# Mixer output read once into the weight buffer, output projection by token chunks, sums of the second norm made during the projection

## What is computed

```
cq, ckv, kr, hq, ... = split_projection(h @ lp['w_in'])     # h: modulated rmsnorm of x
o_mla = rmsnorm(mla_attention(...), lp['mla_out_norm'])     # (T, 512)
o_hg  = rmsnorm(o_hg, ...) * silu(hg)                       # (T, 256), gated linear recurrence
o_gla = rmsnorm(o_gla, ...) * silu(gg)                      # (T, 256), gated linear recurrence
mix = jnp.concatenate([o_mla, o_hg, o_gla], axis=-1) @ lp['w_o']
x = x + g1 * mix
h2 = rmsnorm(x, lp['norm_ffn']) * (1.0 + sc2) + sh2
a, u = jnp.split(h2 @ lp['w_ffn_in'], 2, axis=-1)
x = x + g2 * ((jax.nn.silu(a) * u) @ lp['w_ffn_out'])
```

## Time and profile before

| | us |
|---|---|
| median of 3 runs | 3866.0 (3865.39 to 3866.11) |
| the profiled execution's own time | 3858.27 |
| its span, first to last instruction | 3856.5 |
| TensorE busy | 3408.7 |
| VectorE busy | 1475.6 |
| ScalarE busy | 987.9 |
| GpSimd busy | 674.9 |

### The profile page before, as it was taken

One profiled execution on the slowest core, in us unless ns is written; L12 is line 12 of the kernel. 1 busy time (PEld: TensorE's weight loads), 2 busy tenths in 40 slices (PEclk: granted clock), 3 DMA queues, 4 the chain that ended last, 5 costly groups with the idle time before them and its releaser, 6 DMA issues.

```text
span 3856.5 us, 53744 instructions
## 1 busy us (share of the span) xinstructions
PE 3408.7 (88%) x20827; PEld 3059.2 (79%) x20827; DVE 1475.6 (38%) x2528; ACT 987.9 (26%) x2023; POOL 674.9 (18%) x1041
## 2 busy tenths in 40 slices
PE   4799788988959999999948997889879599999998
PEld 3699556766849999999928985567659499999998
DVE  1511345644333433433424104455442344343343
ACT  2421234432131111111123213344330311111110
POOL 0211556531010000000002126475300100000000
PEclk6899889999879999999958998899979799999999
DMA  6144111101200111110141441111021011011111
GB/s 225 43 151 145 53 48 61 38 16 63 78 22 33 44 54 33 54 44 33 33 143 69 153 137 54 44 48 36 18 94 54 11 43 55 33 47 51 33 33 47
DMA packets 194358, 238.29 MB, mean 62 GB/s; under 512 B 20582, under 2 KB 168316, under 8 KB 194204
## 3 DMA queue, kind: packets, MB, share of 16 engines
q1 hardware_dynamic: 163992, 184.07, 15.1%
q0 software_dynamic: 11232, 31.97, 2.4%
q10 hardware_dynamic: 18980, 20.14, 1.7%
HBM read 196.06 MB, written 40.08 MB: 61 GB/s over the span
## 4 chain that ended last, share of the span: by engine, by line
PE 82%; DVE 5%; POOL 3%; ACT 3%; issue 3%; DMA 2%; ACTq 1%; SPq 0%; DVEq 0%; POOLq 0%
PE banks L1282 78%; PE banks L1278 4%; DVE probs_t L2110 1%; ACTq L875 1%; ACT norm_t L858 1%; DVE norm_t L1863 1%; DMA mix_token_major<-mixer_out 1%; DVE act_split L1871 1%; POOL act_split L555 1%; DVE w_split L1846 0%; ACT probs L1113 0%; POOL r_qb L633 0%; POOL r_kb L626 0%; DVE a_stats L2097 0%; DVE r_qb L2016 0%
## 5 line engine op out<-in xcount | busy, mean ns | idle before, releaser
L1282 PE MATMUL banks<-act_split,w_split 128*128 128x384 f32 (+1 forms) x8352 | 1390.8, 328 | 46.0 <-DVE act_split L1871 36.7
L1282 PEld LDWEIGHTS banks<-act_split,w_split 128*128 128x128 f32 x8352 | 1386.1, 189 | 48.3 <-issue 38.1
L1282 PE MATMUL banks<-hidden_split,w_split 128*128 128x384 f32 (+1 forms) x3168 | 528.0, 327 | 0.0
L1282 PEld LDWEIGHTS banks<-hidden_split,w_split 128*128 128x128 f32 x3168 | 524.7, 188 | 0.7 <-DVE hidden_split L2217 0.3
L1880 DVE SCALAR_TENSOR_TENSOR x<-banks,mod,x 128x384 f32<-128x384 f32 (+2 forms) x768 | 354.2, 496 | 231.1 <-PE banks L1282 229.1
L2214 DVE TENSOR_TENSOR hidden_f<-banks,silu_a 128x384 f32<-128x384 f32 x132 | 70.7, 536 | 780.3 <-PE banks L1282 780.3
L1282 PEld LDWEIGHTS banks<-w_split,act_split 128*128 128x128 f32 (+1 forms) x2592 | 315.8, 182 | 16.6 <-issue 10.7
L1282 PE MATMUL banks<-w_split,act_split 128*128 128x264 f32 (+1 forms) x2592 | 326.6, 285 | 0.0
L555 POOL CAST act_split<-norm_t 128x384 fp32r<-128x384 f32 (+1 forms) x96 | 55.0, 572 | 1386.1 <-ACT norm_t L858 1385.4
L1261 ACT ACTIVATE w_split<-w_raw 128x2048 fp32r<-128x2048 f32 x60 | 112.4, 1905 | 383.9 <-PE banks L1282 383.9
L1255 ACT ACTIVATE hidden_split<-hidden_f 128x384 fp32r<-128x384 f32 x132 | 67.0, 508 | 536.5 <-DVE hidden_f L2214 536.5
(11 more groups left out here) (187 smaller groups left out, 3421.9 us busy)
## 6 DMA issues: line engine op xcount, KB each, us to landing
w_raw<-in_w_ffn_in SPq DMA_DIRECT2D x44, 1024.0 KB, 5.1
w_mod_raw<-in_w_mod SPq DMA_DIRECT2D x34, 1024.0 KB, 5.5
w_raw<-in_w_ffn_out SPq DMA_DIRECT2D x22, 1024.0 KB, 4.9
w_mod_first<-in_w_mod ACTq DMA_DIRECT2D x14, 1024.0 KB, 13.7
z_token_major<-z_stage POOLq DMA_DIRECT2D x96, 132.0 KB, 2.1
w_raw<-in_w_in SPq DMA_DIRECT2D x10, 1056.0 KB, 5.8
r_qkg<-z_feature_major SPq DMA_DIRECT2D x16, 576.0 KB, 4.2
r_v<-z_token_major SPq DMA_DIRECT2D x16, 512.0 KB, 3.5
```

Source lines behind the costliest of these rows:

```text
L1282: return T.matmul(out, lhsT, rhs, start=start, stop=stop, skip_group_check=True)
```

## The change

- SyncE loads `mixer_out` while attention still runs: eight tiles into MT, now in slots 1 and 2 of W, each as soon as its store has landed, and of the last tile the recurrence's half into MTR. The last tile's attention half isn't stored and is turned from OM. GpSimd's last `clear` is left out.
- Split 9 is made in the last attention tile, after head 4's copies.
- TensorE turns tiles in the order `MIX`, into banks 4 to 7, five tiles before the projection, two before q = 1 and two before q = 2.
- In the projection the chunk loop is outside the column-tile loop (q = 6m + 2c + ct). Splits 10 and 11 follow q = 2 on VectorE, 12 to 14 follow q = 5, 11 and 17, and split 15 follows the whole norm.
- ScalarE squares each feature tile as soon as its residual is done, GpSimd adds the squares of a chunk up in ACC, and TensorE multiplies the sum once per chunk (`chunk_sum`): chunk 0 after q = 20, the others after q = 23. Chunk 0 is scaled on ScalarE, VectorE and GpSimd ahead of what these do for q = 21 to 23.
- The FFN's wait for a chunk of the norm stands before that chunk's matmuls, inside the loop.

The diff, cut to its core:

```diff
+MIX = [0, 1, 2, 3, 4, 5, 8, 6, 7]
+SQUARED = [q for q in range(24) if q not in (0, 2, 4)]
+MIX_END = ["m2b", "m5b", "m7b"]
...
-    a = [h_at, h_end]
-    MT = place("mix_token_major", [P, 2, D_MODEL], F32, a)
+    MT = place("mix_token_major", [P, NTILE - 1, D_MODEL], F32, [w_at + SLOT * 8, w_end])
+    MTR = place("mix_last", [P, 512], F32, [lt_at, lt_end])
+    SQN = place("norm_sq_n2", [P, 2, 384], F32, [h_at, h_end])
+    TNN = place("norm_t_n2", [P, 2, 384], F32, [h_at + TOK * 4, h_end])
+    ACC = place("norm_sum", [P, 3, 384], F32, [h_at + TOK * 8, h_end])
...
-                sp.wait_ge(a_out, (l + 1) * NTILE * 16)
-                for t, (t0, n) in enumerate(TILES):
-                    if t == 0:
-                        wait(sp, "a_pe", l, f"PV{ORDER[-1]}_7")
-                        wait(sp, "a_dve", l, f"on{ORDER[-1]}")
-                    if t >= 2:
-                        wait(sp, "mix_pe", l, f"m{t - 2}b")
-                    sp.dma_start(MT[0:n, t % 2], mix_d[t0:t0 + n, :]).then_inc(m_ld[t % 2], 16)
+                wait(sp, "a_dve", l, f"qssb{ORDER[-1]}")
+                t0, n = TILES[ORDER[-1]]
+                sp.dma_start(MTR[:], mix_d[t0:t0 + n, 512:1024]).then_inc(m_ld, 16)
+                for i, t in enumerate(ORDER[:-1]):
+                    t0, n = TILES[t]
+                    sp.wait_ge(a_out, (l * (NTILE - 1) + i + 1) * 16)
+                    sp.dma_start(MT[0:n, i], mix_d[t0:t0 + n, :]).then_inc(m_ld, 16)
...
-                out(NTILE - 1)
-                norm_hi("n2", l)
...
+                def add(q):
+                    c, d = q % 6 // 2, 2 * (q // 6) + q % 2
+                    cn = CHUNKS[c][1]
+                    if d:
+                        wait(pool, "n2_act", l, f"sq{q}")
+                        if d > 1:
+                            wait(pool, "n2_pool", l, f"ad{q - 1 if q % 2 else q - 5}")
+                        s.done(V.tensor_tensor(ACC[:, c, 0:cn], ACC[:, c, 0:cn], SQN[:, SQUARED.index(q) % 2, 0:cn], ALU.add),
+                               f"ad{q}")
+
+                def high(c):
+                    c0, cn = CHUNKS[c]
+                    for k in range(KT8):
+                        wait(pool, "n2_act", l, f"h{c}{k}")
+                        s.done(V.tensor_copy(A[:, 0, k, c0:c0 + cn], TNN[:, k % 2, 0:cn]), f"hi{c}{k}")
+
+                for q in range(21):
+                    add(q)
+                high(0)
+                for q in range(21, 24):
+                    add(q)
+                high(1)
+                high(2)
...
+                        if not more and h == 4:
+                            split_hi(l, 9, lambda: wait(act, "r_dve", l, "out8"), 12)
...
+                def square(q):
+                    c, d = q % 6 // 2, 2 * (q // 6) + q % 2
+                    c0, cn = CHUNKS[c]
+                    wait(act, "wo_dve", l, f"o{q}")
+                    out = ACC[:, c, 0:cn]
+                    if d:
+                        j = SQUARED.index(q)
+                        out = SQN[:, j % 2, 0:cn]
+                        if j >= 2:
+                            wait(act, "n2_pool", l, f"ad{SQUARED[j - 2]}")
+                    s.done(S.activation(out, X[:, d, c0:c0 + cn], ACT.Square), f"sq{q}")
+
+                def scaled(c):
+                    cn = CHUNKS[c][1]
+                    wait(act, "n2_pe", l, f"q{c}")
+                    if c:
+                        wait(act, "n2_dve", l, f"t{c - 1}7")
+                    s.done(S.activation(RS[:, 0:cn], ps[6 + c % 2][:, 0:cn], ACT.Ln, bias=EPSC), f"rl{c}")
+                    wait(act, "n2_act", l, f"rl{c}")
+                    s.done(S.activation(RS[:, 0:cn], RS[:, 0:cn], ACT.Exp, scale=-0.5), f"rs{c}")
...
+                for q in range(6, 12):
+                    square(q)
+                split_hi(l, 13, lambda: wait(act, "wo_pe", l, "o11"), 16)
+                for q in range(12, 18):
+                    square(q)
+                split_hi(l, 14, lambda: wait(act, "wo_pe", l, "o17"), 17)
+                for q in range(18, 21):
+                    square(q)
+                scaled(0)
+                for q in range(21, 24):
+                    square(q)
+                scaled(1)
+                scaled(2)
+                split_hi(l, 15, lambda: wait(act, "wo_pe", l, "o23"), 18)
...
+                def mix_turn(t):
+                    n = TILES[t][1]
+                    if t == ORDER[-1]:
+                        wait(pe, "a_dve", l, f"on{t}")
+                    for b in range(2):
+                        i = 2 * MIX.index(t) + b
+                        if i >= 4:
+                            wait(pe, "mix_dve", l, f"m{MIX[i // 2 - 2]}{'ab'[b]}")
+                        src = (OM, MTR)[b] if t == ORDER[-1] else MT[:, ORDER.index(t), 512 * b:512 * b + 512]
+                        for k in range(4):
+                            ins = transpose(ps[4 + i % 4][:, P * k:P * k + n], src[0:n, P * k:P * k + P], CST[0:n, 0:n])
+                        st("mix_pe").done(ins, f"m{t}{'ab'[b]}")
+
+                def chunk_sum(c):
+                    cn = CHUNKS[c][1]
+                    wait(pe, "n2_pool", l, f"ad{19 + 2 * c}")
+                    if c == 2:
+                        wait(pe, "n2_act", l, "rl0")
+                    st("n2_pe").done(mm(ps[6 + c % 2][:, 0:cn], CST[:, O_ONES:O_ONES + P], ACC[:, c, 0:cn], True, True), f"q{c}")
+
+                for t in MIX[:5]:
+                    mix_turn(t)
                 s = st("wo_pe")
-                wait(pe, "mix_dve", l, "m8b")
                 for m in range(4):
                     split_ready(9 + m)
                     w = W[:, (9 + m) % 3, :, 0:2048].rearrange("p a (k c) -> p a k c", k=8)
-                    for ct in range(2):
-                        for c, (c0, cn) in enumerate(CHUNKS):
-                            q = 6 * m + 3 * ct + c
+                    for c, (c0, cn) in enumerate(CHUNKS):
+                        for ct in range(2):
+                            q = 6 * m + 2 * c + ct
+                            if q in (1, 2):
+                                mix_turn(MIX[3 + 2 * q])
+                                mix_turn(MIX[4 + 2 * q])
+                            if m == 0 and ct == 0:
+                                wait(pe, "mix_dve", l, MIX_END[c])
                             if q >= 6:
                                 wait(pe, "wo_dve", l, f"o{q - 6}")
                             for k in range(KT8):
...
                                     ins = mm(ps[q % 6][:, 0:cn], w[:, wa, k, P * ct:P * ct + P], A[:, xa, k, c0:c0 + cn],
                                              k == 0 and j == 0, k == KT8 - 1 and j == 2)
                             s.done(ins, f"o{q}")
+                            if q == 20:
+                                chunk_sum(0)
+                chunk_sum(1)
                 wait(pe, "wo_dve", l, "o23")
-                norm("n2", l)
-
-
-                for c in range(3):
-                    wait(pe, "n2_dve", l, f"lo{c}7")
+                chunk_sum(2)
...
+                                wait(pe, "n2_dve", l, f"lo{c}7")
...
+                for i in range(10):
+                    mix_low(i)
+                for q in range(3):
+                    project(q)
+                    if q < 2:
+                        for i in range(10 + 4 * q, 14 + 4 * q):
+                            mix_low(i)
+                for m in range(10, 12):
                     split_lo(l, m, m + 3)
...
-                norm("n2", l, 32, 56)
+                for q in range(3, 6):
+                    project(q)
+                split_lo(l, 12, 15)
+                for q in range(6, 12):
+                    project(q)
+                split_lo(l, 13, 16)
+                for q in range(12, 18):
+                    project(q)
+                split_lo(l, 14, 17)
+                for q in range(18, 21):
+                    project(q)
+                scaled(0)
+                for q in range(21, 24):
+                    project(q)
+                scaled(1)
+                scaled(2)
+                split_lo(l, 15, 18)
```

More of the change, by code:

```diff
@@ L814, in _ @@
                         elif h == 7:
-                            if q:
+                            if q and more:
                                 clear(q)
-                            else:
+                            elif not q:
                                 wait(pool, "a_pe", l, f"S{ORDER[0]}_7")
@@ L1236, in _ @@
                     split_hi(l, m, lambda: None, m + 3)
-                split_hi(l, 12, lambda: wait(act, "wo_pe", l, "o5"), 15)
-                for j in range(3):
-                    split_hi(l, 13 + j, lambda: wait(act, "wo_pe", l, f"o{[11, 17, 23][j]}"), 16 + j)
-                norm("n2", l, 24)
+                s = st("n2_act")
+                def square(q):
[9 more added lines that the diff above has]
+                    s.done(S.activation(out, X[:, d, c0:c0 + cn], ACT.Square), f"sq{q}")
@@ L2180, in _ @@
```

(45 more changed lines are left out.)

35 lines of the change are left out of this document (25 added, 10 removed).

## The result

The changed kernel takes 3715.25 us (median of 4, 3710.81 to 3718.05) against 3865.69 us for the kernel before (median of 4, 3862.02 to 3866.11): a ratio of 0.9612 (0.9595 to 0.9628), 150.4 us less. The forecast was 3724, with a range of 3708 to 3746. The profiled execution took 3713.52, 144.8 less than the profiled one of before.

A forecast was written before the change was run, and what follows sets the result against it. TensorE, busy 88% of the span, was taken as the bound, so gains come only from its idle stretches around the projection: 71.0 us per layer, 142 in two, off 3866.0 gives 3724 us, range 3708 to 3746.

The forecast's parts named there:

- step 2: Last attention tile: split 9 made there holds attention up by 2.1 us per layer (bounds 0 and 2.3).
- T: End of q = 20 in the projection, forecast at 1045.0 us in layer 0, 11.2 us before the projection ends.
- step 3: From attention's end to the projection: ten half tiles turned first, start moved from 982.96 to 955.6 us.
- step 4: Projection: matmuls stay at 96.7 us, and eight half tiles turned between them add 3.9 us (bounds 3.4 and 7.3).
- step 5: Norm by chunks beside projection and FFN: the FFN's second column tile begins 52.7 us after T.
- p = 3: Start of the FFN's second column tile, forecast to move from 1168.66 to 1097.7 us, 71.0 us per layer.
- Step 1: Nine mixer output loads issued during attention, costed at nothing, covered by the last tile's attention.
- Rival (b): Mixer loads are late and turns go at their pace: 14 us per layer, 3752 us; chance 0.08.
- the ring: Attention's cycle per head: scores, row maximum on VectorE, exponential on ScalarE, next head's scores; 4.80 us in the last tile.
- Rival (d): Projection, broken up by transposes, runs at 1.2 GHz: 96.7 us longer per layer, 3917 us; chance 0.01.
- that sign of being wrong: In the FFN: an A part of a later group taking more than its 47.56 us would show the prediction wrong.
- Rival (a): Norm application slower as engines and adds share memory: 12 to 15 us per chunk, 9 per layer, 3742 us; chance 0.15.

The follow-up runs named there:

- the changed kernel's second run: The changed kernel measured again with nothing altered, on one chip with three follow-up runs: 3713.39 us, 0.961 of the kernel before.
- the run with both edits: Changed kernel with split 9's subtraction on GpSimd, residuals 21 and 22 inside chunk 0's scaling, and chunk 1's sum after q = 22: 3701.91 us.

## Why the prediction was right

The mechanism was right, and of the terms most were close. The misses went both ways, and that the total gain of 147.9 us came within 6 of the forecast's 142 is in part luck: step 2 cost 5.1 us more than forecast in the two layers together, and steps 3 to 5 gave 10.2 more. Per layer, in us (T taken as the start of the first sum):

| | predicted | layer 0 | layer 1 |
|---|---|---|---|
| step 2: last tile longer by | 2.1 | 2.6 | 6.7 |
| step 3: end of attention to projection | 8.1 | 8.3 | 7.5 |
| step 4: projection to T | 89.4 | 87.2 | 87.2 |
| step 5: T to p = 3 | 52.7 | 50.0 | 50.0 |
| gain up to p = 3 | 71.0 | 75.3 | 72.6 |

The terms account for both gains; in layer 1 the kernel before also had 0.7 us more between attention and projection to lose.

**Step 1, loads at no cost:** right (the bytes were 4.0 MB with the last tile's half, not 3.75, which changes nothing). No transpose waits for a DMA, and taking the cover away costs 25 us. Rival (b) is refuted; its 14 us per layer was a fair price for the uncovered case (12.9).

**Step 2, the split in attention:** the term was mis-sized. VectorE in layer 0:

```profile
938.70 2.29 DVE L1944 TENSOR_TENSOR w_split<-w_raw,w_split 128x2048 fp32r<-128x2048 f32 x1 [1.88 <-ACT w_split L865]
940.90 1.22 DVE L2195 TENSOR_REDUCE a_stats<-banks 128x1 f32<-128x1024 f32 x1
```

As predicted, the subtraction waits for ScalarE's copy and the row maximum starts when it ends. TensorE stands still for 1.90 us there, where the heads before have 0.19, so 1.7 us are the ring's own delay, where 2.1 was forecast. The prediction took that delay for the whole price and left out what the clock does after the stop. It looked for one head of 6.9 us; the row maxima are 6.50 and then 5.77 us apart in layer 0, 6.50 and 6.85 in layer 1. The windows of the changed kernel (us, busy by engine with counts, granted clock, DMA share, GB/s):

```profile
940.00:943.00 3.00, 1.10 (x10) 0.86 (x10) 3.00 (x4) 0.84 (x1) 0.00 (x0) 1.00 0.22 61
943.00:947.00 4.00, 4.00 (x15) 2.30 (x15) 0.65 (x2) 0.36 (x2) 0.00 (x0) 0.69 0.61 217
947.00:951.00 4.00, 4.00 (x35) 4.00 (x34) 2.81 (x4) 1.21 (x2) 0.00 (x0) 0.88 0.00 0
...
957.30:961.70 4.40, 4.40 (x23) 4.33 (x24) 4.08 (x7) 2.89 (x6) 0.00 (x0) 0.61 0.00 0
961.76:966.00 4.24, 4.24 (x27) 4.22 (x26) 1.46 (x3) 0.88 (x2) 0.00 (x0) 1.00 0.02 6
...
1080.20:1084.00 3.80, 3.80 (x14) 3.80 (x15) 2.61 (x6) 2.61 (x6) 0.93 (x2) 0.61 0.00 0
...
1091.70:1098.90 7.20, 7.19 (x49) 7.20 (x50) 4.37 (x5) 4.16 (x7) 0.00 (x0) 1.00 0.43 144
2770.00:2775.00 5.00, 4.97 (x14) 2.80 (x15) 0.58 (x1) 0.62 (x2) 0.00 (x0) 0.57 0.55 191
2775.00:2781.00 6.00, 6.00 (x32) 6.00 (x31) 2.74 (x4) 1.21 (x2) 0.00 (x0) 0.51 0.00 0
```

After the stop the clock falls to the 1.2 GHz level, for part of the two windows up to 951.00 in layer 0 (0.69 and 0.88) and for nearly all of 11 us in layer 1 (0.57 and 0.51), and the scores of the next head take 2.91 and 3.73 us where they took 1.94 for the head before. That is the other 0.9 and 5.0 us. Over all runs with VectorE's split in attention the last tile took 41.9 to 48.0 us, and 39.0 to 39.5 in all without it. The prediction had itself found such a fall, and didn't apply it to this stop.

**Step 3:** right within 0.6 us; VectorE's subtractions and the transposes at half clock (24 in 4.71; 3.87 in layer 1) share the pace.

**Step 4:** 2.2 us better in both layers. The 96.7 us of the kernel before held a cold start of its own, which the prediction carried over: 16 chunks of 4.20 and 8 of 3.50 are 95.2. Now the projection begins at a granted clock of 1.00, and its first 24 matmuls take 966.01 - 961.76 = 4.25 us: 1.5 us. The turned half tiles took 1.61 us (966.01 to 967.62) and 1.67 (971.90 to 973.57), 3.3 in place of 3.9. Rival (d), half clock through the projection, didn't occur: from 973.60 to 1048.90 the granted clock was 1.00.

**Step 5:** 2.7 us better. In us after T, with the predicted value in brackets: chunk 0 from 2.4 to 14.3 (2.5 to 14.5), the gap before chunk 1's sum 4.46 (some 5), chunk 1 from 19.3 to 31.1 (19.7 to 31.7), first FFN matmuls at 19.1 (20.6), chunk 2 done at 42.6 (43.8). Chunk 0's first multiplications and last subtraction:

```profile
1051.36 1.03 DVE L2318 TENSOR_TENSOR norm_t_n<-x,norm_rs 128x384 f32<-128x384 f32 x2 [1.62 <-ACT norm_rs L1289]
...
1062.61 0.56 DVE L2307 TENSOR_TENSOR act_split<-norm_t_n,act_split 128x384 fp32r<-128x384 f32 x1 [0.40 <-POOL act_split L844]
```

Since the FFN started 1.5 us sooner, it stood 2.15 us before chunk 1 and 1.32 before chunk 2, where 1 and 3.6 were forecast. The first of these restarts was cold (10.20 for 8.40) and the second warm: one cold start among the two, as in the sum, but with chunk 2 itself costing 7.2, not 8.8. With the 1.1 us by which it began sooner, that makes the 2.7. The A parts of the FFN's later groups took 47.56 us, as before, so that sign of being wrong didn't show.

**Rival (a)** is true as a mechanism and wasn't on the path. In the change the adds run when VectorE isn't in the norm, so a chunk takes 11.8 us. The runs that overlap them show the price, 1.23 us for 0.56. By the Trainium skill (GPSIMD Engine Reference, Key points) GpSimd and VectorE share SBUF interfaces and contend where VectorE has two inputs in SBUF; the traces agree, both here and where VectorE reads PSUM and wasn't slowed.

**What stays open.** Why the same 1.90 us stop costs 0.9 us of slow clock in one layer and 5.0 in the other (and up to 7 in another run) isn't settled; the traces show the length and not the cause. The length of a stop doesn't decide it alone. The restart behind the 2.04 us stop at the turned tiles went at 0.61 here and at 1.00 in layer 0 of the changed kernel's second run (948.94 to 952.50). In layer 1 of that run the FFN's restart behind 1.82 us kept 1.00. Behind 2.90 us the run with both edits had 0.80 and 0.68 in layer 0 (1083.78 to 1090.00) and 1.00 in layer 1. Which restart of a run comes out cold is in part chance, then, and no forecast from rows like these can be exact there.

## What to carry to other kernels

Work put into an engine's gap costs what it delays in the ring that this engine serves, and, if TensorE stops for some 2 us by it, a stretch at half clock on top (0.9 to 7 us here); an idle engine that is half as fast (GpSimd's 4.51 us for 2.29) can be the better place. Before moving an instruction off a wait, look at what stands behind it in TensorE's order: the wait of the next sum took back nearly all of it here. Two more buffers for a tile that goes round through three engines paid 8 us here, and part of the waits came back as longer instructions.

## What the hardware showed that wasn't expected

- In the changed kernel's profiled run TensorE's clock fell after stops of 1.90 us (both layers), 2.04 and 2.15 us, but not after one of 1.32 (1.00 in the window 1091.70 to 1098.90); other runs kept 1.00 after 2.04 and 2.90 us, so no length found here divides the two cases. The Trainium skill (TensorE: Matmul & The Clock Gate, section on the HAM clock gate) has half speed as the default; the restart after 1.32 us shows that a stop can leave the full clock, so not each restart is cold.
- In the window 940.00 to 943.00 the clock was still 1.00 in spite of the stop in it, and 0.69 in the next four microseconds, when TensorE was busy throughout: the loss came after the stop, not in it.
- Transposes alone brought the clock back: with the loads late, 40 of them behind 14.03 us of idleness began at 0.50, and the projection behind them had 1.00 (973.08 to 977.30). In the change 24 of them at 0.61 were followed by a projection at 1.00 from its first microsecond, while after 4.81 us of idleness without transposes its first 24 matmuls took 6.65 us.
- Two-input instructions of VectorE and GpSimd slow each other. GpSimd's first add, beside VectorE's splits 10 and 11, took 2.59 us, the others of its size 1.01, and two splits that start right behind each other took 5.30 together where one takes 2.29. The times fit an engine that waits for the other's whole instruction: the first split ends at 978.55 + 2.29 = 980.84, and an add of 1.01 from there ends at 981.85, where it ended at 981.71 (an estimate from these rows; no run was made on it). GpSimd and VectorE of the changed kernel:

```profile
979.12 2.59 POOL L837 TENSOR_TENSOR norm_sum<-norm_sum,norm_sq_n 128x384 f32<-128x384 f32 x1 [63.52 <-ACT norm_sq_n L1280]
985.02 1.01 POOL L837 TENSOR_TENSOR norm_sum<-norm_sum,norm_sq_n 128x384 f32<-128x384 f32 x1 [3.32 <-ACT norm_sq_n L1280]
...
978.55 5.30 DVE L1944 TENSOR_TENSOR w_split<-w_raw,w_split 128x2048 fp32r<-128x2048 f32 x2
```
